# Order of VectorE's work in a slot that holds a pair of heads: the convolution moved behind the weights and the former pair's outputs

## The chip, the cores and the metric

One core of one Trainium2 chip runs the kernel. The metric is device time in microseconds (us) of one launch, the median of several runs; lower is better.

## The reference

One step of a hybrid decoder layer over a prompt of 256 tokens and 8 samples of 8 tokens each, 320 tokens in all (`T = 320`), in float32. After a SwiGLU feed-forward block, a projection `w_in` feeds two branches: an mLSTM and a Mamba-2 scan (SSD). Both are merged, projected, and followed by a second feed-forward block. The change is in the SSD branch:

```python
xbc, sconv1 = _causal_conv(xbc, sconv0, p['s_conv_w'], p['s_conv_b'])   # 4 taps, 3072 channels
xbc = jax.nn.silu(xbc)            # x (2048 channels), B and C (4 groups x 128 each)
...
cum = jnp.cumsum(dtc * A, axis=1)
lmat = jnp.exp(jnp.where(mask, cum[:, :, None] - cum[:, None, :], -jnp.inf))
xdt = xc * dtc[..., None]
cb = jnp.einsum('btgn,bsgn->btsg', cc, bc)
y = (jnp.einsum('btsg,btsge,bsgep->btgep', cb, lmat, xdt)
     + jnp.exp(cum)[..., None] * jnp.einsum('btgn,bgepn->btgep', cc, h))
h_new = (jnp.exp(cum[:, -1])[..., None, None] * h
         + jnp.einsum('bsgn,bsge,bsgep->bgepn', bc, decay, xdt))
```

There are 32 heads of 64 channels in 4 groups of 8 heads; the state has 128 columns. Two heads share one tile of 128 channels, a *pair*, so a group is four pairs.

## The kernel before

**Layout.** Activations lie channels-first, 128 channels a tile on the partitions and 320 tokens in the free dimension. Weights stream from HBM in panels of 1 MB through a ring of four buffers (`ring`), two *units* to a panel. A unit is one tile of 128 output channels.

**A dense unit** (`dense`, L841) multiplies in two halves for float32 accuracy. ScalarE rounds the unit's weights to `w_hi` (`high_ahead`, L1512, instruction L1522), VectorE computes the rest `w_lo` (`low_ahead`, L2076, instruction L2085), and TensorE does 8 matmuls `w_hi` by `u_hi`, 8 `w_hi` by `u_lo`, and 8 `w_lo` by `u_hi`, all through L820. Both halves have two buffers and are made two units ahead: in the slot of unit u, ScalarE waits until TensorE is done with u, then makes the high half of u+2, and VectorE follows with the low half of u+2. A ring buffer is refilled by SyncE once the last low half of its panel is made.

**Groups and slots.** While the SSD scan of a group runs, the remaining units of the projection run between its steps. The loop `for gr in range(SG)` with an inner loop over the eight units of a phase (`phase_units`) stands, in the same shape, in the program of every engine: TensorE L1388, ScalarE L1941, GpSimd L771, VectorE L2669. One pass of the inner loop is a *slot*, i = 0 to 7. There is no planner: each engine's program order is written out by hand, and engines meet on semaphores. In groups 0, 1 and 2 the units of slots 0 to 3 are `xbc` units, which need a convolution; in group 3 these are `gb` units, which need none. Slots 4 to 7 hold `ga` or `z` units (a gate).

**What each engine does in a slot:**
- TensorE: the dense unit; in slot 0 the transposes of the group's inputs and the B-by-C scores (`group_rows`, L1278); in slots 0 to 3 the decay rows of pair i (`decay_rows`, L1304, two matmuls of 448 columns into `aux`); in slot 1, for gr > 0, the transposes of the old part; in slot 2 the growth factors (`grown_decays`, from L2609's tile); in slots 1 to 4 the outputs of pair i - 1 (`head_outputs`, L1316), which wait for that pair's weights (`w_ready`); in slots 4 to 7 the state work (`sample_states`, L1350). The first of these, in slot 4, waits for VectorE to have read all four pairs' outputs (`y_read`), since the state updates go into the same PSUM banks 2 and 3.
- ScalarE: the high half; in an `xbc` slot the copy of the unit's result from PSUM into a padded row `pad2` (L1508; three buffers, reused after the convolution three units before is done); in slots 0 to 3 the exponentials of pair i from `aux` into `w_int` (`head_weights`, L1912, instructions L1923 to L1925, twice); four slots after each `xbc` unit its SiLU (`conv_silu`, L1661), from `acc2` (four buffers).
- GpSimd: history columns and tails of the padded row (`conv_side`, L656), and the selectors of the next pair (`picks`, L762).
- VectorE: the low half (L2085); `conv` (L2241): four chained instructions over 344 columns, L2253, twice L2255, L2257, into `acc2`; in slot 0 `group_rows` (L2580, instructions L2587 to L2594) and `masked_scores` (L2612, L2618 to L2621); in slot 1 `old_part` (for gr > 0; L2664, L2666) and `sample_masks` (L2597; L2602, L2604, and L2609, which feeds TensorE's growth factors); in slots 0 to 3 `weights` of pair i (L2623; L2630 and L2632, which wait for the exponentials and signal `w_ready`); in slots 1 to 4 `outputs` of pair i - 1 (L2635; L2638, signals `y_read`); from slot 4 on `weighted_inputs` (L2644), `update` of the states (L2653) and `gated` (L2525).

`conv` waits for the unit's PSUM bank to be copied out (`bank_free`), for GpSimd's history columns (`hist_put`) and for the SiLU of the unit four before (`conv_silu`).

Of the kernel before, what the change touches and what calls it, by code (L numbers as in the profile page):

```python
# [78 lines left out]
class Stream:  # L79
# [44 lines left out]
    def range(self, first, last):  # L124

        return self.units[self.at[first].n:self.at[last].n + 1]
# [55 lines left out]
def build(nc, io, out):  # L182
# [5 lines left out]
    with ctx:  # L188
# [93 lines left out]
        def part(off, *shape):  # L282
            n = 1
            for s in shape:
                n *= s
            used[0] = max(used[0], off + n)
            assert off + n <= ARENA, off + n
            v = arena[:, off:off + n]
            if len(shape) == 2:
                v = v.rearrange("p (a b) -> p a b", b=shape[1])  # L290
            if len(shape) == 3:
                v = v.rearrange("p (a b c) -> p a b c", b=shape[1], c=shape[2])
            return v
# [63 lines left out]
        pad2 = part(17920, 3, PADW)  # L357
        acc2 = part(18961, 4, PADW)
# [112 lines left out]
        def place(u):  # L471

            return u.own if u.name == "qk" else 16 + (u.own + 8) % 24

        def phase_units(gr):
            return [st.at[name, q] for name, q in four_each(PHASE_UNITS[gr])]
# [1585 lines left out]
        def _(dve):  # L2062
# [13 lines left out]
            def low_ahead(u, last=units[-1]):  # L2076

                done = sum(1 for v in units[:u.n + 1] if v.split)
                while lows[0] < min(done + AHEAD, len(st.split_units)):
                    v = st.split_units[lows[0]]  # L2080
                    if v.n > last.n:
                        break
                    r = v.split_no % 2
                    dve.wait_ge(S["hi_done"], v.split_no + 1)
                    V.tensor_tensor(w_lo[r][:, 0:v.kc, :], panel_part(v), w_hi[r][:, 0:v.kc, :].bitcast(FP32), ALU.subtract)\  # L2085
                        .then_inc(S["lo_done"], 1)
                    lows[0] += 1
# [153 lines left out]
            def conv(u, padded, depth, accs, b_col, w_col, tiles):  # L2241
                own, c = u.own, place(u)
                r = (c - (0 if u.name == "qk" else 16)) % depth
                dve.wait_ge(bank_free[u.bank], u.freed)
                dve.wait_ge(S["hist_put"], c + 1)
                if c >= 4:
                    dve.wait_ge(S["conv_silu"], c - 3)
                a, p = accs[:, c % 4, 0:CONVW], padded[:, r, :]
                if u.name == "qk":
                    dve.wait_ge(S["tap_done"], c + 1)  # L2250
                c = own
                if u.name != "qk":
                    ch.link(V.tensor_scalar(a, p[:, 0:CONVW], par[:, c + w_col:c + w_col + 1], par[:, c + b_col:c + b_col + 1], ALU.mult, ALU.add))  # L2253
                for tap in (1, 2):
                    ch.link(V.scalar_tensor_tensor(out=a, in0=p[:, tap:tap + CONVW], scalar=par[:, c + w_col + tap * tiles:c + w_col + tap * tiles + 1],  # L2255
                                                   in1=a, op0=ALU.mult, op1=ALU.add))
                V.scalar_tensor_tensor(out=a, in0=p[:, 3:3 + CONVW], scalar=par[:, c + w_col + 3 * tiles:c + w_col + 3 * tiles + 1],  # L2257
                                       in1=a, op0=ALU.mult, op1=ALU.add).then_inc(S["conv_done"], 1)
# [263 lines left out]
            def gated(u, dst):  # L2522
                dve.wait_ge(bank_free[u.bank], u.freed)
                c = one(dst, u.own)
                V.tensor_tensor(c, c, one(gate_tmp, gate_no[u.n] % 2), ALU.mult).then_inc(S["gate_used"], 1)  # L2525
# [46 lines left out]
            for q in XBC_FIRST:  # L2572
                u = st.at["xbc", q]
# [6 lines left out]
            def group_rows(gr):  # L2580

                dt = sp[:, :, 4 + 8 * gr:12 + 8 * gr].unsqueeze(3)
                if gr > 0:
                    dve.wait_ge(S["ph_mm"], gr)
                for blk in range(2):
                    dve.wait_ge(S["xt_mm"], 3 * gr + blk + 1)
                    V.tensor_tensor(xd[:, blk, :].rearrange("p (e q) -> p e q", q=64), aux[2 + blk][:, :].rearrange("p (e q) -> p e q", q=64),  # L2587
                                    dt[:, blk].to_broadcast([128, 8, 64]), ALU.mult).then_inc(S["xt_read"], 1)
                dve.wait_ge(S["xt_mm"], 3 * gr + 3)
                if gr > 0:  # L2590
                    dve.wait_ge(S["up_mm"], 4 * gr)
                x = banks[2][0:64, :].rearrange("p (e q) -> p e q", q=64)
                V.tensor_tensor(xd_s[0:64, :].rearrange("p (e q) -> p e q", q=64), x, dt[0:64, 2].to_broadcast([64, 8, 64]), ALU.mult).then_inc(S["xt_read"], 1)
                V.tensor_tensor(xw_s[0:64, :].rearrange("p (e q) -> p e q", q=64), x, sp2[0:64, 2, 8 * gr:8 * gr + 8].unsqueeze(2).to_broadcast([64, 8, 64]),  # L2594
                                ALU.mult).then_inc(S["xt_read"], 1)
# [16 lines left out]
            def masked_scores(gr):  # L2612

                dve.wait_ge(S["cb_mm"], gr + 1)
                if gr > 0:
                    dve.wait_ge(S["w_ready"], 4 * gr)
                blocks = banks[3][:, 0:384].rearrange("p (c t) -> p c t", t=128)
                ch.inc(V.tensor_tensor(cbm[:, 0:384].rearrange("p (c t) -> p c t", t=128)[:, 0::2, :], blocks[:, 0::2, :],  # L2618
                                       tri_m.unsqueeze(1).to_broadcast([128, 2, 128]), ALU.mult))
                ch.inc(V.tensor_copy(cbm[:, 128:256], banks[3][:, 128:256]))  # L2620
                V.tensor_tensor(cbm[0:64, 384:448], banks[3][0:64, 384:448], tri_sm, ALU.mult).then_inc(S["cb_read"], 1)  # L2621
# [13 lines left out]
            def outputs(gr, i):  # L2635
                c = 4 * gr + i
                dve.wait_ge(S["y_mm"], c + 1)
                V.scalar_tensor_tensor(out=xbc_t[:, c, :], in0=xbc_t[:, c, :], scalar=h_dec[:, 128 + c:129 + c], in1=banks[2 + i % 2][:, 0:T],  # L2638
                                       op0=ALU.mult, op1=ALU.add).then_inc(S["y_read"], 1)

            def weighted_inputs(gr):
                dve.wait_ge(S["y_mm"], 4 * gr + 4)
                x = xd[:, :, :].rearrange("p c (e q) -> p c e q", q=64)
                V.tensor_tensor(x, x, sp2[:, 0:2, 8 * gr:8 * gr + 8].unsqueeze(3).to_broadcast([128, 2, 8, 64]), ALU.mult).then_inc(S["xw_ready"], 1)  # L2644
# [13 lines left out]
            def old_part(gr):  # L2658

                dve.wait_ge(S["yi_tr"], gr + 1)  # L2660
                dve.wait_ge(S["grown_read"], gr + 1)
                y = xbc_t[:, 4 * gr:4 * gr + 4, TP:T].rearrange("p t (g s) -> p g t s", g=2)
                o = y_int[:, :, :].rearrange("p g (t s) -> p g t s", s=32)
                ch.link(V.tensor_tensor(o, aux[3][:, 0:256].rearrange("p (g t s) -> p g t s", g=2, s=32),  # L2664
                                        grown.rearrange("p (t g s) -> p g t s", g=2, s=32), ALU.mult))
                V.tensor_tensor(y, y, o, ALU.add).then_inc(S["yi_add"], 1)  # L2666
                dve.wait_ge(S["yi_add"], gr + 1)

            for gr in range(SG):  # L2669
                for i, u in enumerate(phase_units(gr)):  # L2670
                    low_ahead(u)
                    if u.name == "xbc":
                        conv(u, pad2, 3, acc2, 216, 240, 24)
                    if i == 0:
                        group_rows(gr)
                        masked_scores(gr)
                    if i == 1:
                        if gr > 0:
                            old_part(gr - 1)
                        sample_masks(gr)  # L2680
                    if i < 4:
                        weights(gr, i)
                    if 1 <= i <= 4:
                        outputs(gr, i - 1)
                    if i == 4:
                        weighted_inputs(gr)
                    if i >= 4:
                        update(gr, i - 4)
                        gated(u, ya if u.name == "ga" else xbc_t)
# [111 lines left out]
```

## Time and profile before

| | |
|---|---|
| median of 3 runs | 1363.53 us |
| lowest, highest | 1362.2, 1368.29 us |
| the profiled execution: time, span | 1357.09 us, 1355.3 us |
| its mean granted TensorE clock | 0.979 of full speed |
| TensorE (PE) busy | 1278.2 us |
| VectorE (DVE) busy | 767.9 us |
| ScalarE (ACT) busy | 617.8 us |
| GpSimd (POOL) busy | 216.4 us |

The span runs from the first to the last instruction of the one execution that was profiled; its time has the launch around it as well. Times in rows below are us from the start of the span. The four groups of the SSD scan lie at about 727 to 789, 789 to 845, 845 to 900 and 900 to 956 us. The last five lines are shares of one execution with many stages; what a wait in one stage costs has to be read in that stage.

How the rows are read: a timeline row gives start, duration, engine, line, operation, the tile written and the tiles read with their shapes, how many instructions are merged (x), and in brackets how long the engine sat idle before it and which instruction released it. PE is TensorE's matmul queue and PEld its weight loads. All matmuls of the kernel have line 820 and all transposes line 817, as they go through one helper. Tiles that are cut from one large allocation all have the name `arena`; PSUM tiles are `bank` and `aux`. An instruction's shown end can lie a few hundredths of a microsecond behind the start of the next on the same engine.

### The profile page before, as it was taken

To read this page: it belongs to the slowest core of one execution; us is meant where nothing else is said; L and a number is where in the kernel's file an instruction comes from. 1 tells how busy PE (TensorE), PEld (TensorE's weight loads), DVE (VectorE), ACT (ScalarE), POOL (GpSimd) and SP (SyncE) were. 2 spreads that over 40 slices of the span, in tenths; PEclk is the share of its full clock that TensorE was granted. 3 is DMA by queue.
4 is the path that set the end of the run, shared out by engine and by line. 5 is a ranking of instruction groups with operands and counts; after the bars stand their busy time and mean duration, and the time that the engine had idled before them with its cause. 6 is when DMAs were issued, how large, how long until landed. Compare 5 with 4: busy or idle time off the path is not lost.

```text
span 1355.3 us, 22662 instructions
## 1 busy us (share of the span) xinstructions
PE 1278.2 (94%) x9096; PEld 1161.7 (86%) x9096; DVE 767.9 (57%) x1340; ACT 617.8 (46%) x1067; POOL 216.4 (16%) x377
## 2 busy tenths in 40 slices
PE   5899999998999898999999989999999999999997
PEld 2799999997988666778998878788899979999997
DVE  1644445336874455755389676865466565545433
ACT  3433334334667454544355664554563343333342
POOL 4100000002541211111033232321410010000010
PEclk9899999998999999999999999999989999999998
DMA  9957776785332778783673435463335465444551
GB/s 306 257 187 229 234 229 197 226 244 165 124 110 94 250 263 296 253 283 119 173 218 125 139 119 166 138 210 118 116 97 156 155 198 172 141 145 136 150 148 41
DMA packets 258862, 241.56 MB, mean 178 GB/s; under 512 B 8607, under 2 KB 242479, under 8 KB 258710
## 3 DMA queue, kind: packets, MB, share of 16 engines
q1 hardware_dynamic: 249262, 211.03, 50.7%
q0 software_dynamic: 9024, 28.91, 6.1%
q8 instruction: 73, 1.20, 0.4%
q10 hardware_dynamic: 472, 0.17, 0.1%
q14 instruction: 31, 0.25, 0.1%
HBM read 209.88 MB, written 30.21 MB: 177 GB/s over the span
## 4 chain that ended last, share of the span: by engine, by line
PE 57%; DVE 5%; ACT 4%; issue 3%; POOL 1%; DMA 1%; ACTq 0%; DVEq 0%; POOLq 0%
PE bank L820 50%; PE aux L820 6%; ACT w_hi L1522 1%; ACT arena L1508 1%; DVE w_lo L2085 1%; PE aux L817 1%; DVE arena L2255 1%; POOL arena L789 1%; PE bank L817 0%; DMA arena<-in_state_mlstm_C 0%; DMA out_p_C<-arena 0%; ACT L1876 0%; ACT arena L1876 0%; DVE arena L2587 0%; DVE arena L2630 0%
## 5 line engine op out<-in xcount | busy, mean ns | idle before, releaser
L2085 DVE TENSOR_TENSOR w_lo<-ring,w_hi 128x1024 fp32r<-128x1024 f32 (+1 forms) x264 | 336.9, 1277 | 427.9 <-ACT w_hi L1522 427.6
L1522 ACT ACTIVATE w_hi<-ring 128x1024 fp32r<-128x1024 f32 (+1 forms) x264 | 289.4, 1097 | 554.7 <-PE bank L820 548.9
L820 PE MATMUL bank<-u_hi,w_hi 128*128 128x320 f32 x1536 | 277.7, 324 | 6.9 <-ACT u_hi L1547 5.1
L820 PEld LDWEIGHTS bank<-u_hi,w_hi 128*128 128x128 f32 x1536 | 240.5, 195 | 24.5 <-issue 18.8
L820 PE MATMUL bank<-u_lo,w_hi 128*128 128x320 f32 x1536 | 259.1, 312 | 0.0
L820 PE MATMUL bank<-u_hi,w_lo 128*128 128x320 f32 x1536 | 256.6, 309 | 0.0
L820 PEld LDWEIGHTS bank<-u_lo,w_hi 128*128 128x128 f32 x1536 | 236.6, 190 | 0.0
L820 PEld LDWEIGHTS bank<-u_hi,w_lo 128*128 128x128 f32 x1536 | 233.8, 188 | 0.0
L622 POOL TENSOR_TENSOR arena<-arena 128x320 f32<-128x320 f32 x24 | 21.0, 874 | 607.7 <-ACT arena L1534 596.7
L817 PE MATMUL aux<-ident,arena 128*128 128x128 f32 (+6 forms) x404 | 60.3, 274 | 15.9 <-ACT arena L1579 8.8
L820 PE MATMUL bank<-arena 32*128 32x128 f32 (+5 forms) x536 | 55.2, 377 | 16.5 <-issue 6.8
L817 PEld LDWEIGHTS aux<-ident,arena 128*128 128x128 f32 (+6 forms) x404 | 45.1, 142 | 26.9 <-issue 15.1
L820 PE MATMUL bank<-ff_hi,w_hi 128*128 128x320 f32 x352 | 58.5, 314 | 0.0
L820 PEld LDWEIGHTS bank<-arena 32*128 32x128 f32 (+3 forms) x536 | 29.8, 155 | 32.6 <-issue 20.4
L820 PE MATMUL bank<-ff_lo,w_hi 128*128 128x320 f32 x352 | 56.8, 309 | 0.0
L820 PE MATMUL bank<-ff_hi,w_lo 128*128 128x320 f32 x352 | 56.8, 309 | 0.0
L820 PEld LDWEIGHTS bank<-ff_hi,w_hi 128*128 128x128 f32 x352 | 52.3, 188 | 2.5 <-issue 2.5
L820 PEld LDWEIGHTS bank<-ff_hi,w_lo 128*128 128x128 f32 x352 | 52.9, 188 | 0.0
L820 PEld LDWEIGHTS bank<-ff_lo,w_hi 128*128 128x128 f32 x352 | 52.9, 188 | 0.0
L2255 DVE SCALAR_TENSOR_TENSOR arena<-arena,par 128x344 f32<-128x344 f32 x80 | 46.5, 581 | 7.3 <-POOL arena L669 5.1
L820 PE MATMUL aux<-arena 128*32 128x128 f32 (+3 forms) x360 | 46.7, 345 | 4.0 <-ACT arena L1508 3.1
L1508 ACT ACTIVATE arena<-bank 128x256 f32<-128x256 f32 (+4 forms) x138 | 44.4, 352 | 11.9 <-PE bank L820 8.5
(362 smaller groups left out, 1515.4 us busy)
## 6 DMA issues: line engine op xcount, KB each, us to landing
ring<-in_w_in SPq DMA_DIRECT2D x52, 1024.0 KB, 5.1
ring<-in_ff_w SPq DMA_DIRECT2D x44, 1024.0 KB, 5.3
ring<-in_ada_w SPq DMA_DIRECT2D x36, 1024.0 KB, 7.8
ring<-in_ff_w SPq DMA_DIRECT2D x32, 704.0 KB, 4.7
arena<-in_state_mlstm_C SPq DMA_DIRECT2D x32, 512.0 KB, 4.3
out_s_C<-arena POOLq DMA_DIRECT2D x32, 512.0 KB, 4.8
ring<-in_w_pa SPq DMA_DIRECT2D x8, 1024.0 KB, 7.6
arena<-in_state_ssm SPq DMA_DIRECT2D x32, 256.0 KB, 3.4
```

Of the source, the lines that this page charges most:

```text
L622: ins = nc.gpsimd.tensor_tensor(sq[:, 0, :], sq[:, 0, :], sq[:, kc, :], ALU.add)
L789: ch.link(nc.gpsimd.tensor_tensor(gsq[gr][:, 0:2, :], gsq[gr][:, 0:2, :], gsq[gr][:, 2:4, :], ALU.add))
L817: return nc.tensor.transpose(dst, src, ident[0:rows, 0:rows])
L820: return nc.tensor.matmul(dst, lhs, rhs, start=first, stop=last)
L1508: return nc.scalar.activation(dst, src, ACT.Copy, scale=scale)
L1522: nc.scalar.activation(w_hi[v.split_no % 2][:, 0:v.kc, :], panel_part(v), ACT.Copy).then_inc(S["hi_done"], 1)
L2085: V.tensor_tensor(w_lo[r][:, 0:v.kc, :], panel_part(v), w_hi[r][:, 0:v.kc, :].bitcast(FP32), ALU.subtract)\
L2255: ch.link(V.scalar_tensor_tensor(out=a, in0=p[:, tap:tap + CONVW], scalar=par[:, c + w_col + tap * tiles:c + w_col + tap * tiles + 1], in1 ...
```

## The change

In VectorE's slot the convolution no longer stands behind the low half but behind the outputs of the former pair. Nothing else is changed; no instruction is added or removed.

```diff
@@ -2669,8 +2669,6 @@
             for gr in range(SG):
                 for i, u in enumerate(phase_units(gr)):
                     low_ahead(u)
-                    if u.name == "xbc":
-                        conv(u, pad2, 3, acc2, 216, 240, 24)
                     if i == 0:
                         group_rows(gr)
                         masked_scores(gr)
@@ -2682,6 +2680,8 @@
                         weights(gr, i)
                     if 1 <= i <= 4:
                         outputs(gr, i - 1)
+                    if u.name == "xbc":
+                        conv(u, pad2, 3, acc2, 216, 240, 24)
                     if i == 4:
                         weighted_inputs(gr)
                     if i >= 4:
```

## Rows read from the trace of the kernel before

**Rows 1.** The page's first part: busy us, share of the span, instructions.

```profile
PE 1278.2 (94%) x9096; PEld 1161.7 (86%) x9096; DVE 767.9 (57%) x1340; ACT 617.8 (46%) x1067; POOL 216.4 (16%) x377
```

**Rows 2.** Source view of L2632, then L2638, 728 to 875: waits for them (us, times).

```profile
  PE bank L820: 5.5, 8
...
  PE bank L820: 0.9, 3
```

**Rows 3.** Timeline of TensorE, second group, slots 1 to 5.

```profile
798.33 0.87 PE L820 MATMUL bank<-arena 128*64 128x256 f32 x8 [1.06 <-DVE arena L2632]
...
803.92 0.69 PE L820 MATMUL aux<-w_lo_rest,parity 32*128 32x256 f32 x2 [0.34 <-DVE w_lo_rest L2609]
804.99 0.87 PE L820 MATMUL bank<-arena 128*64 128x256 f32 x8 [0.38 <-DVE arena L2632]
...
815.60 0.87 PE L820 MATMUL bank<-arena 128*64 128x256 f32 x8 [0.58 <-DVE arena L2632]
...
818.05 1.16 PE L820 MATMUL bank<-arena 32*128 32x128 f32 x16 [0.28 <-DVE arena L2638]
...
819.71 1.44 PE L820 MATMUL bank<-u_hi,w_hi 128*128 128x320 f32 x8
```

**Rows 4.** Timeline of TensorE, first group, slots 1 and 4.

```profile
737.49 0.87 PE L820 MATMUL bank<-arena 128*64 128x256 f32 x8 [0.88 <-DVE arena L2632]
...
753.90 0.87 PE L820 MATMUL bank<-arena 128*64 128x256 f32 x8 [0.57 <-DVE arena L2632]
...
756.35 1.16 PE L820 MATMUL bank<-arena 32*128 32x128 f32 x16 [0.29 <-DVE arena L2638]
```

**Rows 5.** Timeline of VectorE: slot 0 of the first group, slots 0 to 4 of the second.

```profile
729.59 1.23 DVE L2085 TENSOR_TENSOR w_lo<-ring,w_hi 128x1024 fp32r<-128x1024 f32 x1 [1.58 <-ACT w_hi L1522]
...
790.51 1.22 DVE L2085 TENSOR_TENSOR w_lo<-ring,w_hi 128x1024 fp32r<-128x1024 f32 x1 [5.92 <-ACT w_hi L1522]
791.65 0.47 DVE L2253 TENSOR_SCALAR arena<-arena,par 128x344 f32<-128x344 f32 x1
...
793.88 1.28 DVE L2587 TENSOR_TENSOR arena<-aux,sp 128x512 f32<-128x512 f32 x2
...
797.12 0.96 DVE L2630 SCALAR_TENSOR_TENSOR arena<-arena 128x768 f32<-128x768 f32 x1
...
811.03 1.23 DVE L2085 TENSOR_TENSOR w_lo<-ring,w_hi 128x1024 fp32r<-128x1024 f32 x1 [0.75 <-ACT w_hi L1522]
...
816.22 1.23 DVE L2085 TENSOR_TENSOR w_lo<-ring,w_hi 128x1024 fp32r<-128x1024 f32 x1 [0.21 <-ACT w_hi L1522]
817.36 0.54 DVE L2638 SCALAR_TENSOR_TENSOR arena<-arena,h_dec,bank 128x320 f32<-128x320 f32 x1
```

**Rows 6.** Timeline of ScalarE: last exponentials of slots 0 (first, second group) and 3.

```profile
734.90 0.31 ACT L1925 ACTIVATE arena<-aux,g 64x64 f32<-64x64 f32 x1
...
795.34 0.31 ACT L1925 ACTIVATE arena<-aux,g 64x64 f32<-64x64 f32 x1
...
812.68 0.32 ACT L1925 ACTIVATE arena<-aux,g 64x64 f32<-64x64 f32 x1
```

**Rows 7.** Timeline of the fourth group: VectorE in slot 0, TensorE in slot 4.

```profile
906.68 0.96 DVE L2630 SCALAR_TENSOR_TENSOR arena<-arena 128x768 f32<-128x768 f32 x1 [0.90 <-ACT arena L1925]
...
927.05 1.16 PE L820 MATMUL bank<-arena 32*128 32x128 f32 x16 [0.93 <-DVE arena L2638]
```

**Rows 8.** Windows: length, busy us (x) of PE, PEld, DVE, ACT, POOL, PEclk, DMA, GB/s.

```profile
726.00:732.50 6.50, 4.30 (x30) 3.52 (x29) 4.75 (x8) 2.76 (x8) 3.23 (x8) 1.00 0.51 163
...
770.20:773.80 3.60, 2.12 (x26) 1.76 (x23) 2.25 (x6) 3.31 (x5) 0.08 (x1) 1.00 0.62 176
773.80:777.20 3.40, 3.40 (x25) 2.72 (x26) 1.44 (x6) 2.29 (x4) 1.50 (x2) 0.50 1.02 298
```

**Rows 9.** Timeline of TensorE, first group, slot 6.

```profile
773.80 1.15 PE L820 MATMUL aux<-arena 128*32 128x128 f32 x16 [1.48 <-ACT arena L1508]
774.88 2.48 PE L820 MATMUL bank<-u_hi,w_hi 128*128 128x320 f32 x8
```

## The prediction

> **What bounds the kernel now.** The page's first part comes first: TensorE is busy 94% of the span, VectorE 57% [rows 1], so a VectorE order can only matter where TensorE stands still for it. The source view of the two VectorE lines that TensorE waits for here says how much that is: over the three groups whose slots hold a convolution it waits 5.5 us in 8 waits for the weights (L2632) and 0.9 us in 3 for the outputs (L2638) [rows 2]. The timeline places them. In the second group (gr 1) TensorE waits 1.06 us in slot 1, 0.34 and 0.38 us in slot 2 (first for the decay rows of L2609, then for the weights), nothing in slot 3, and 0.58 and 0.28 us in slot 4 [rows 3]; in the first group 0.88, 0, 0, then 0.57 and 0.29 us [rows 4]. The third group's weights waits are what is left of 5.5 us, 5.5 - 0.88 - 0.57 - 1.06 - 0.38 - 0.58 = 2.0 us, so it repeats the second, and I take its L2609 wait as 0.34 too. All together: first group 1.74, second and third 2.64 each, 7.0 us in all.
>
> The VectorE timeline says why [rows 5]. From the split-off low half at 790.51 to the outputs of pair 3 at 817.36 it runs back to back except for two gaps, 0.75 and 0.21 us, each while it waits for ScalarE's high half. VectorE has hardly any slack in slots 0 to 4.
>
> **What the change moves.** Twelve convolutions (three groups, slots 0 to 3) of four instructions: from the start of the first to the start of what follows, 793.88 - 791.65 = 2.23 us each [rows 5]. Nothing is added or removed; no DMA and nothing of another engine moves. In slot 0 the convolution goes behind the group's rows, the masked scores and the weights; in slot 1 behind the old part, the masks, weights and outputs; in slots 2 and 3 behind weights and outputs. Everything it used to precede starts up to 2.23 us earlier, unless another thing is late next.
>
> Late next: the weights need ScalarE's exponentials. *Slot 0, second group.* Group rows would start at 791.65, and the step from their start to the weights is 797.12 - 793.88 = 3.24 us, so the weights could start at 794.89; but the last exponential ends at 795.34 + 0.31 = 795.65 [rows 6]. So they start at about 795.70: 1.42 us earlier than 797.12, with a new wait of 0.81 us. The fourth group, which has no convolution and so already has the new order, shows this wait: 0.90 us before its first weights [rows 7]. TensorE's 1.06 us in slot 1 goes whole. *Slot 1.* No new wait: the exponentials of pair 1 were made long before. The low half comes first, then the old part, masks and L2609, which end 1.42 us earlier, as do the weights of pair 1. TensorE is itself 1.06 us earlier, so of its 0.72 us in slot 2 0.36 go (1.42 - 1.06) and 0.36 stay. TensorE now runs 1.42 us earlier. *Slots 2 and 3.* The low half of slot 3 stays at about 811.0 (its gap of 0.75 closes, the new wait of slot 0 takes its place), and the weights follow it directly, at 811.0 + 1.1 = 812.1, one convolution earlier than now; their exponentials, earlier by TensorE's 1.42 us, end at 812.68 + 0.32 - 1.42 = 811.6 [rows 6], in time. The 0.58 us of slot 4 goes: TensorE is 2.00 us earlier.
>
> *Slot 4 is where it is given back.* There TensorE, after its transposes, waits for the outputs of pair 3, because the state updates overwrite the same PSUM banks. Those outputs come after the low half of slot 4, and that after convolution 3. So before the outputs of pair 3 stands the same VectorE work as before, in another order, and their time moves only by the change in its waits. Before: the gaps of 0.75 and 0.21 us; as an instruction starts some 0.07 us before the last one's shown end where nothing is waited for, they cost 0.82 and 0.28, together 1.10 us. After: both close, since the convolution fills them, and the 0.80 us in slot 0 is new. Outputs of pair 3: 817.36 - 1.10 + 0.80 = 817.06, 0.30 us earlier. TensorE reaches this wait 2.00 us earlier and leaves it 0.30 us earlier: the wait grows from 0.28 to 0.28 + 2.00 - 0.30 = 1.98 us. The third group is the same. *First group:* the low half starts at 729.59 [rows 5], group rows could start 1.14 later at 730.73, weights 3.24 later at 733.97, but the exponentials end at 734.90 + 0.31 = 735.21 [rows 6]; new wait about 1.28 us. The two gaps there are as in the second, cost 1.1. Outputs of pair 3: 0.17 us later; TensorE arrives 0.88 + 0.57 = 1.45 us earlier and the wait grows from 0.29 to 0.29 + 1.45 + 0.17 = 1.91 us.
>
> **Sum:** +0.17 - 0.30 - 0.30 = -0.4 us, against the profiled execution's 1357.1 us: 1356.7. That execution is 6.4 us below the median of the three runs, 1363.53; the difference of 0.4 us carried over gives **1363.1 us**.
>
> Costed at nothing, with the cover: the low halves of slots 1 to 3 start up to 1.3 us later (first group, slot 1), but each is for the unit two slots on, and a slot is over 5 us; cover gone, it would cost that 1.3 us once a group. SyncE refills a ring buffer after its last low half, so its loads leave as much later, into a ring of four panels with eight units in it. GpSimd and ScalarE reuse the padded rows three convolutions later, and the SiLU of a convolution comes four slots on. Each has more than a slot over against at most 5 us. Bounds: the wait on the exponentials could be 0 at best (group rows slower to start) and 1.3 us at worst in all three, which gives -0.8 x 2 - 1.28 = -2.9 us more on one side and +1.0 us on the other.
>
> **A price the sum leaves out: the clock.** The stalls were spread, none over 1.06 us; now one of about 2 us stands in front of small matmuls (32 rows). Two stretches bear on it. From 726.00 to 732.50 TensorE was busy 4.30 of 6.50 us, with a long wait inside, and its granted clock stayed 1.00 (2.4 GHz). From 770.20 to 773.80 it was busy 2.12 of 3.60 us, and the clock then stood at 0.50 (1.2 GHz) for the 3.4 us to 777.20 [rows 8]. Just before that fall stood a wait of 1.48 us beside small matmuls, and a second stretch like it, some 10 us on, went the same way. The new slot 4 has a wait of 1.98 us and then the small matmuls of the row at 818.05 [rows 3]. Price of one fall: eight dense matmuls took 2.48 us [rows 9] where 1.44 us is usual [rows 3], at least 1.0 us; 3.4 us at half speed lose 1.7 us, the upper end.
>
> The Trainium skill, "TensorE: Matmul & The Clock Gate", section "HAM oscillation — how this bites in real kernels", warns that an array left waiting between bursts is throttled again and the next tile starts cold. That speaks against this change; the trace agrees at 773.8 and not in the stretch from 726. [...]
>
> **Rivals.**
> 1. *Waits swapped, clock holds* (forecast): -0.4 us, 1363.1 us. For it: the VectorE work before pair 3's outputs is the same. Chance 0.48.
> 2. *Clock falls, the slower side.* Place: slot 4 of one to three groups, at the long wait for pair 3's outputs. It decides from a wait like the 1.48 us ones on; before, none in slot 4 is over 0.93 us. One fall: -0.4 + 1.0 = +0.6; three: -0.4 + 3 x 1.7 = +4.7 us; 1364.1 to 1368.2 us. For it: both falls. Against: the 6.5 us stretch that held, and the head outputs and transposes just before the new wait. Chance 0.38.
> 3. *Gain kept.* If the wait for pair 3's outputs does not stretch. It has a floor: in the fourth group, with no convolution, TensorE still waits 0.93 us there [rows 7], since high half, low half and outputs follow one another. So at most 7.0 - 3 x 0.93 = 4.2 us: 1359.3 us. Against it: convolution 3 is in front of that chain. Chance 0.12.
> 4. *The change does nothing:* one engine executes in program order, so the rows must move; only 0.02 that compiled order differs: 1363.5 us.
>
> **Numbers.** No case comes to 0.5% (6.8 us, about what a measurement of this kernel can tell from no change). Only the runs' own scatter does: 1362.2 to 1368.3 among the three, 1357.1 for the profiled one. So same 0.93; faster 0.03 (case 3 and a low median); slower 0.04 (case 2 with three falls and a high one). Range: from case 3 less some scatter, 1358.0, to case 2's top and some scatter, 1370.0.
>
> **What would show it.** Right: in the changed profile TensorE's waits for L2632 fall from 5.5 to under 1.5 us and those for L2638 rise from 0.9 to about 5.9 us, one near 2 us in slot 4 of each of three groups; VectorE waits for L1925 before the first weights, 0.8 to 1.3 us; the fourth group unchanged. The stretch from the first transposes of a group to the first dense matmul of slot 5 (789.16 to 819.71 in the second) is the same within 0.5 us, or 1.0 to 1.7 us longer with a granted clock below 1.00. Wrong: waits for L2638 that stay at 0.3 to 0.9 us, a new wait for the convolutions on ScalarE or GpSimd, or low halves that TensorE waits for.

## The result and the profile after

| | before | after |
|---|---|---|
| median | 1362.2 us (13 runs, 1356.7 to 1368.3) | 1369.9 us (13 runs, 1358.4 to 1376.4) |
| ratio, 95% interval | | 1.0057 (1.0039 to 1.0076) |
| profiled execution, span | 1355.3 us | 1364.3 us |
| its granted clock | 0.979 | 0.976 |

The change makes the kernel slower by 0.57%, some 7.7 us; the forecast was -0.4 us.

The source view of the same two VectorE lines as in [rows 2], changed kernel, first to third group; who waited (us, times):

```profile
  PE bank L820: 0.8, 2
...
  PE bank L820: 6.5, 3
```

The waits for the weights (L2632) fell from 5.5 to 0.8 us, and those for the outputs (L2638) rose from 0.9 to 6.5 us. The timeline of TensorE, changed kernel, slots 1 to 5 of the second group and a bit of the first and third (columns as in [rows 3]):

```profile
757.78 1.16 PE L820 MATMUL bank<-arena 32*128 32x128 f32 x16 [2.16 <-DVE arena L2638]
...
797.36 0.87 PE L820 MATMUL bank<-arena 128*64 128x256 f32 x8
...
803.81 0.87 PE L820 MATMUL bank<-arena 128*64 128x256 f32 x8 [0.38 <-DVE arena L2632]
...
813.77 0.87 PE L820 MATMUL bank<-arena 128*64 128x256 f32 x8
...
818.08 1.74 PE L820 MATMUL bank<-arena 32*128 32x128 f32 x16 [2.15 <-DVE arena L2638]
819.74 1.08 PE L820 MATMUL aux<-arena 128*32 128x128 f32 x16
820.76 2.50 PE L820 MATMUL bank<-u_hi,w_hi 128*128 128x320 f32 x8
823.06 2.33 PE L820 MATMUL bank<-u_lo,w_hi 128*128 128x320 f32 x8
...
876.51 2.08 PE L820 MATMUL bank<-arena 32*128 32x128 f32 x16 [2.15 <-DVE arena L2638]
```

The waits of 1.06, 0.34 and 0.58 us in [rows 3] are gone, 0.38 us stays, and 0.28 us has become 2.15 us, once in each group. The new part stands behind that wait: in the second group the eight dense matmuls at 820.76 take 2.50 us, where the row at 819.71 in [rows 3] has 1.44. The windows view of the changed kernel (columns as in [rows 8]) has the clock: 1.00 during the wait, 0.53 and 0.50 in the two stretches after it, and 1.00 in the first group, whose wait was as long:

```profile
757.80:762.00 4.20, 4.20 (x49) 3.88 (x50) 3.53 (x10) 1.48 (x3) 0.30 (x1) 1.00 0.01 4
814.70:818.30 3.60, 1.45 (x16) 1.18 (x16) 3.53 (x6) 3.44 (x7) 0.00 (x0) 1.00 0.70 243
818.30:821.80 3.50, 3.50 (x36) 2.86 (x35) 2.71 (x9) 0.00 (x0) 0.00 (x0) 0.53 0.00 0
821.80:825.20 3.40, 3.40 (x15) 3.40 (x14) 0.61 (x2) 0.00 (x0) 1.50 (x2) 0.50 0.34 100
```

VectorE, changed kernel, first group, slot 0, the end of slot 3 and slot 4: the convolution is off the front, and the weights wait for the exponentials instead.

```profile
734.76 0.21 DVE L2621 TENSOR_TENSOR arena<-bank,w_lo_rest 64x64 f32<-64x64 f32 x1
736.34 0.96 DVE L2630 SCALAR_TENSOR_TENSOR arena<-arena 128x768 f32<-128x768 f32 x1 [1.38 <-ACT arena L1925]
...
753.76 0.45 DVE L2253 TENSOR_SCALAR arena<-arena,par 128x344 f32<-128x344 f32 x1
...
755.96 1.22 DVE L2085 TENSOR_TENSOR w_lo<-ring,w_hi 128x1024 fp32r<-128x1024 f32 x1
757.09 0.54 DVE L2638 SCALAR_TENSOR_TENSOR arena<-arena,h_dec,bank 128x320 f32<-128x320 f32 x1
```

The last three rows are the order that was foreseen: convolution 3, the low half, and only then the outputs that TensorE waits for.

### The profile page after: what moved, and what is told of

Read it like the earlier page. It is cut to its first block and busy times, and to the rows that moved or that the text cites. A ratio compares the mean times of both kernels' runs of the same rounds, so it can differ in the third digit from the quotient of the medians.

```text
span 1364.3 us, 22662 instructions
## 1 busy us (share of the span) xinstructions
PE 1282.2 (94%) x9096; PEld 1165.6 (85%) x9096; DVE 768.3 (56%) x1340; ACT 617.7 (45%) x1067; POOL 209.4 (15%) x377
## 5 line engine op out<-in xcount | busy, mean ns | idle before, releaser
L1508 ACT ACTIVATE arena<-bank 128x256 f32<-128x256 f32 (+4 forms) x138 | 44.4, 352 | 11.9 <-PE bank L820 8.5
```

The costliest lines, as they stand in the source:

```text
L1508: return nc.scalar.activation(dst, src, ACT.Copy, scale=scale)
```

## The experiments

Two numbers are used for each kernel beside its ratio: the mean granted clock over its runs, and from it the time that half speed costs. A mean clock of c over T us means T x (1 - c) us lost, an estimate from above, since half speed during a wait costs nothing. For the kernel before this is 1362.1 x (1 - 0.9781) = 29.8 us (35 runs, beside the first four experiments), for the changed one 1369.4 x (1 - 0.9744) = 35.1 us (13 runs). So of the 7.3 us between these means 5.3 us is clock. The stretches below are called *the groups*, from the first transposes of the first group to the end of TensorE's first wait for one of GpSimd's group sums (728.66 to 959.98 before, 729.76 to 966.01 in the changed kernel), and *the tail*, from there to the end of the span. The time also follows the clock from run to run: of the 13 of the changed kernel the fastest (1358.4 us) had the highest clock, 0.981, and the slowest (1376.4 us) 0.972.

**Filler in the wait.** TensorE, in `sample_states`, first three groups:

```diff
                 if j == 0:
+                    if gr < SG - 1:
+                        nxt = phase_units(gr)[5]
+                        pe.wait_ge(bank_free[nxt.bank], nxt.uses)
+                        for _ in range(12):
+                            mm(bank_of(nxt), u_hi[:, 0, 0:128], u_hi[:, 0, :])
                     pe.wait_ge(S["y_read"], 4 * gr + 4)
```

> The changed kernel, with 12 filler matmuls (320 columns, into the PSUM bank of the next unit, overwritten by it) in TensorE's program just before its wait for pair 3's outputs in slot 4 of the first three groups. Twelve take about 1.8 us where the wait is 2.15 us, so they hide in it. Theory A (the long wait makes the granted clock fall, the waits themselves are only swapped): the clock stays 1.00 through slot 4 and the time comes back to that of the kernel before within 2 us (ratio 1.000, -0.4 to +1 us). Theory B (the loss of 7.7 us is in waits or in other engines' work, whatever the clock): ratio stays near 1.0057.

Measured: 1360.1 us, ratio 0.998 (0.9966 to 0.9993), mean clock 0.9790. VectorE's program is that of the changed kernel; only what TensorE does while it waits is different. Its timeline, first group, slot 4 (five lines more in the file, so L2643 is the outputs' L2638):

```profile
756.76 2.01 PE L820 MATMUL bank<-u_hi 128*128 128x320 f32 x12
759.08 1.16 PE L820 MATMUL bank<-arena 32*128 32x128 f32 x16 [0.31 <-DVE arena L2643]
760.17 0.65 PE L820 MATMUL aux<-arena 128*32 128x128 f32 x16
760.74 1.43 PE L820 MATMUL bank<-u_hi,w_hi 128*128 128x320 f32 x8
```

The state matmuls come as late as before the filler went in, yet the dense ones behind them run at 1.43 us, and no slot 4 in this profile has a clock below 1.00. The whole loss is gone. Theory B falls: its 1.0057 is far outside the interval. The time is even 1.9 us below that of before, where theory A's sum has -0.4 us. Of the 9.6 us between the means of this kernel and the changed one 6.5 us are clock (35.1 - 28.6); the other 3 us are taken up below.

**The wait in another place.** VectorE, slot 3's convolution put back:

```diff
                     low_ahead(u)
+                    if u.name == "xbc" and i == 3:
+                        conv(u, pad2, 3, acc2, 216, 240, 24)
...
-                    if u.name == "xbc":
+                    if u.name == "xbc" and i < 3:
                         conv(u, pad2, 3, acc2, 216, 240, 24)
```

> The changed kernel, but the convolution of slot 3 stands where it was, behind the low half; slots 0 to 2 keep the new order. VectorE has the same work in front of pair 3's outputs, so TensorE's total wait in slot 4 stays about 2 us, but 1.9 us of it should stand before the head outputs (L2632), behind dense matmuls, and almost none before the small state matmuls. Theory A' (it takes a long wait joined to the small matmuls for the clock to fall): time within 2 us of before. Theory A'' (any wait of 2 us in this stretch is enough): ratio 1.004 to 1.006. Theory B: ratio 1.0057.

Measured: 1362.95 us, ratio 1.001 (0.9995 to 1.0025), mean clock 0.9785. TensorE's timeline, second group, slot 4:

```profile
820.42 0.87 PE L820 MATMUL bank<-arena 128*64 128x256 f32 x8 [2.00 <-DVE arena L2632]
821.22 0.33 PE L820 MATMUL bank<-arena,xd_s 64*64 64x64 f32 x4
821.48 1.10 PE L817 MATMUL aux<-ident,arena 128*128 128x128 f32 x8
822.56 1.16 PE L820 MATMUL bank<-arena 32*128 32x128 f32 x16
823.65 0.65 PE L820 MATMUL aux<-arena 128*32 128x128 f32 x16
824.23 1.43 PE L820 MATMUL bank<-u_hi,w_hi 128*128 128x320 f32 x8
```

A wait of 2.00 us, nearly as long, but with dense matmuls ahead of it and head outputs and transposes behind. The clock held. So the length alone does not decide; a wait joined to the small state matmuls does what this one does not. In the other two groups it is the same, with waits of 2.02 and 2.00 us. A' is right, A'' wrong.

**Slot 3 alone.** The kernel before, only the convolution of slot 3 moved:

```diff
-                    if u.name == "xbc":
+                    if u.name == "xbc" and i < 3:
                         conv(u, pad2, 3, acc2, 216, 240, 24)
...
+                    if u.name == "xbc" and i == 3:
+                        conv(u, pad2, 3, acc2, 216, 240, 24)
```

> The kernel before with only the convolution of slot 3 moved behind the weights and outputs; slots 0 to 2 in the old order. The weights waits of slots 1 and 2 stay (0.9 to 1.06, 0.34 and 0.38 us), the 0.58 us one of slot 4 goes, and the wait for pair 3's outputs is about 0.9 us instead of 0.28. Theory A: a wait of 0.9 us is as in the fourth group, where the clock held, so the time is that of before within 2 us. Theory B (an inherent cost of running the convolution of slot 3 late, for example for slots 4 to 7): ratio 1.004 or more.

Measured: 1364.4 us, ratio 1.0023 (1.0004 to 1.0041), mean clock 0.9781. Between the two theories, because the wait was mis-sized: 1.48 us, not 0.9, since the weights of slot 3 now wait for their exponentials (0.78 us), a wait that I had left out. Second and third group, slot 4:

```profile
819.64 1.16 PE L820 MATMUL bank<-arena 32*128 32x128 f32 x16 [1.48 <-DVE arena L2638]
...
821.30 1.44 PE L820 MATMUL bank<-u_hi,w_hi 128*128 128x320 f32 x8
...
875.67 1.16 PE L820 MATMUL bank<-arena 32*128 32x128 f32 x16 [1.48 <-DVE arena L2638]
...
877.34 2.13 PE L820 MATMUL bank<-u_hi,w_hi 128*128 128x320 f32 x8
```

The same wait cost a fall in one of these groups and none in the other, nor in the first group, where it is 1.48 us too. The runs' mean clock is not below that of before, so this small loss (2.5 us) is not shown to be the clock's; what else it may be comes below.

**Outputs first in slot 4.**

```diff
+                    if i == 4:
+                        outputs(gr, 3)
                     low_ahead(u)
+                    if i == 4 and us[3].name == "xbc":
+                        conv(us[3], pad2, 3, acc2, 216, 240, 24)
...
-                    if 1 <= i <= 4:
+                    if 1 <= i < 4:
                         outputs(gr, i - 1)
-                    if u.name == "xbc":
+                    if u.name == "xbc" and i < 3:
                         conv(u, pad2, 3, acc2, 216, 240, 24)
```

> The changed kernel, and in slot 4 the outputs of pair 3 go first, ahead of the low half, and the convolution of slot 3 behind that low half. Pair 3's outputs then follow TensorE's head outputs at once, so the wait in slot 4 should be under 0.3 us in every group, the fourth one too, where it was 0.93. Waits that go: about 1.7 us in the first group, 2.3 in the second and third, 0.9 in the fourth. Theory A: 7 us faster than before, ratio 0.995, granted clock not below that of before. Theory B (a late convolution costs by itself): little better than the changed kernel.

Measured: 1356.6 us, ratio 0.9957 (0.994 to 0.9973), mean clock 0.9793. In its profile no TensorE wait for L2638 is left in the four groups, only 0.8 us for L2632. It beats both kernels, and with the convolution later than in either, so a late convolution has no large cost by itself. It is 5.3 us faster, a little less than the 7 expected: in slot 4 of each of the four groups TensorE now waits 0.36 us for ScalarE (L1508), 1.4 us in all that the expectation left out.

**Profiles repeated: the changed kernel twice more, the kernel before once more.**

> The changed kernel unaltered, for a second profile. Theory A1 (the clock falls in slot 4 nearly every time): the granted clock is 0.50 for a stretch right after the wait for pair 3's outputs in at least two of the three groups. Theory A2 (the two falls of the first profile were chance): in none or one.

> The changed kernel unaltered, for a third profile, as the one before: A1 two or three falls in slot 4, A2 none or one.

> The kernel before unaltered, for a second profile. Both theories: no fall in slot 4 of any group. It also shows whether the wait of 2.4 us for GpSimd's second group sum in the tail, which the changed kernel's profile has at 973.96 and that of before has not, goes with the kernel or with where the clock falls: with the kernel, it is absent here; with the clock, it appears when the clock does not fall near the first group sum.

Windows of the second profile of the changed kernel (1368.6 us; first group, second group, third group):

```profile
762.90:766.40 3.50, 2.41 (x24) 2.20 (x28) 2.37 (x5) 2.56 (x5) 0.00 (x0) 0.58 0.00 1
766.40:769.80 3.40, 3.40 (x26) 3.00 (x18) 2.27 (x9) 0.00 (x0) 0.96 (x2) 0.50 0.02 5
828.00:832.00 4.00, 4.00 (x33) 3.50 (x30) 2.66 (x10) 0.00 (x0) 0.97 (x2) 0.57 0.00 0
876.00:890.00 14.00, 11.85 (x111) 10.75 (x108) 11.40 (x23) 6.38 (x16) 3.84 (x6) 1.00 0.29 92
```

and of the third (1374.5 us):

```profile
761.50:768.90 7.40, 6.82 (x46) 6.21 (x47) 4.13 (x11) 2.05 (x4) 1.59 (x2) 0.54 0.09 28
826.90:834.20 7.30, 7.30 (x50) 6.66 (x50) 3.38 (x10) 0.00 (x0) 1.50 (x2) 0.53 0.19 56
885.00:892.00 7.00, 6.82 (x47) 6.21 (x48) 3.72 (x11) 0.27 (x2) 1.50 (x2) 0.51 0.11 33
```

Seven of nine slots 4 in three profiles had a fall: two, two, three. Six of these seven lost 3.4 us (two stretches at half speed, 7 us in a row), one lost 1.7 us: 6 x 3.4 + 1.7 = 22.1 us, 7.4 us an execution. The second profile of the kernel before (1360.7 us) had none, as the first. A1 is right. The execution with the most falls is the slowest of the three.

This is not the net cost. The waits of 1.48 us in slots 6 and 7 of the first group had a fall of 1.7 us in four of four places before and in four of six in the changed kernel, 1.1 us an execution less. In all, the groups took 231.3 and 231.6 us before and 236.3, 234.5 and 240.5 us in the changed kernel, 5.7 us more in the mean; the tail took 395.3 and 395.7 us, then 398.3, 396.3 and 398.1 us, 2.1 us more. The stretch ahead of the groups, where the two kernels have the same program, differs by 3.1 us between these means too, so such means of two and three executions are good to a few microseconds.

**More filler.** The kernel of outputs first, with the same kind of filler (9 matmuls in slots 6 and 7 of the first group, 10, 12 and 18 ahead of the three waits for group sums in the tail; `filler` waits for the bank and issues the matmuls, and its definition is left out here):

```diff
...
+                if gr == 0 and j >= 2:
+                    filler((phase_units(0) + phase_units(1))[4 + j + 1], 9)
...
+                    filler(tail_units()[2], 10)
                     group_sums(0)
...
                     group_sums(1)
+                    filler(tail_units()[3], 12)
                     group_sums(2)
...
+                    filler(tail_units()[6], 18)
                     group_sums(3)
```

> The kernel of outputs first in slot 4, and in TensorE's program filler matmuls (as in the filler run, 1.3 to 2.7 us in all each time) ahead of the other long waits of this stretch: slots 6 and 7 of the first group (wait 1.48 us each) and the three waits for GpSimd's group sums in the tail (1.5, up to 2.4, 2.85 us). The fillers compute nothing that is used. Theory A (a long wait costs its own length and a fall of the clock behind it, and matmuls in the wait prevent the fall): four falls fewer of 1.7 us each, so about 6 us less than outputs first alone: 1350 us, ratio 0.991, clock up by 0.005. Theory B (the clock falls do not matter to the time here, other work hides them): 1356 us as before.

Measured: 1354.6 us, ratio 0.9948 (0.9922 to 0.9973), mean clock 0.9835. The falls went, none is left in the groups or near the group sums: the clock is up by 0.0042, 5.7 us. But the time is only 2.0 us below that of outputs first, inside both intervals (1.0 us if each is set against the kernel before beside it). So some 4 us of the 5.7 do not show in the time: theory A's 0.991 lies outside the interval, and theory B's 1356 us inside. What the falls in slots 6 and 7 and in the tail cost is therefore not shown by this run. In the tail of its profile TensorE waits 2.2 us for ScalarE to read a bank (in two waits), which the profile of outputs first has not; but that of the one-group kernel below, which has no filler, has it too, so this is not shown to be the filler's doing. This kernel is no proven gain over outputs first.

**The wait halved.** The changed kernel, and in slot 4 `outputs(gr, 3)` ahead of `low_ahead(u)`, nothing else.

> The changed kernel, and in slot 4 only the low half goes behind the outputs of pair 3 (the convolution of slot 3 stays in front of them). The wait for these outputs shrinks by one low half, 2.15 - 1.13 = 1.0 us in the first three groups, and goes in the fourth. Theory A (falls of the clock come with the length of this wait): no or few falls in slot 4, so the waits' own sum remains: -0.4 - 3 x 1.1 - 0.9 = -4.7 us against before, ratio 0.9965, clock as before (0.978). Theory B (a late convolution of slot 3 is what costs): the falls stay and the ratio is 1.002 or more.

Measured: 1359.8 us, ratio 0.9987 (0.9972 to 1.0002), mean clock 0.9772. The wait was as expected, and so was its slot; second group:

```profile
816.61 1.16 PE L820 MATMUL bank<-arena 32*128 32x128 f32 x16 [1.02 <-DVE arena L2638]
817.70 0.65 PE L820 MATMUL aux<-arena 128*32 128x128 f32 x16
818.27 1.43 PE L820 MATMUL bank<-u_hi,w_hi 128*128 128x320 f32 x8
```

No slot 4 of this profile had a fall, and the 7.7 us loss is gone, which B denied. But -4.7 us was not reached, only -1.2 us. In its profile the groups took 226.3 us, 5.2 us less than before, but the tail 399.4 us, 3.9 us more; what that is comes below. The runs' clock was lower than that of before beside them (0.9788), by 0.0016 or 2.2 us. Where those falls are in the runs without a profile is open.

**One group alone.** The new order in the second group, the old one elsewhere (`gr != 1` in front, `gr == 1` behind).

> The new order in the second group only, the old one in the first and third. Theory A: one place for falls instead of three, so about a third of the 7.7 us: +2.5 us, ratio 1.002 (1.000 to 1.003), mean granted clock lower by 0.0012. Theory B (some fixed cost outside the groups, as in the tail): it comes with the first changed group or not at all, ratio 1.000 or 1.0057.

Measured: 1364.5 us, ratio 1.0026 (1.0008 to 1.0044), mean clock 0.9774 against 0.9788 beside it, 0.0014 lower where 0.0012 was expected. One changed group costs 3.6 us, between a third and a half of the three. Its profile happens to show no fall in the slot 4 that was changed, so the reading rests on the runs' clock and time, not on a row. With it the wait of 2.15 to 2.17 us was followed by a fall in seven of ten places. The clock's part here is 1.9 us (1365 x 0.0014); the other 1.7 us is like the rest of the changed kernel below. Both of theory B's values lie outside the interval.

## Why the prediction was wrong

**The moves were right, row by row.** New wait on the exponentials: 1.28, 0.81 and 0.81 us forecast, 1.38 and 0.90 us in the rows (first and second group). TensorE's waits before slot 4: 0 and 0.36 us forecast, 0 and 0.38 measured. The wait for pair 3's outputs: 1.91 and 1.98 us forecast, 2.16 and 2.15 measured. Fourth group: 0.93 us again.

**The sum was close.** From a group's first transposes to the state matmuls of slot 4: 28.02 us (729.76 to 757.78) for 27.69 (728.66 to 756.35) in the first group, 28.76 (789.32 to 818.08) for 28.89 in the second (789.16 to 818.05), and the third likewise. That is +0.3 and twice -0.1 us: +0.1 us in all for -0.4. The missing tenths are mostly low halves in slots 1 and 3 and weights in slot 3, which take 1.31 and 1.04 us where 1.22 and 0.95 us are usual.

**What failed is the step "A price the sum leaves out: the clock", twice.** First its chance: 0.38 for falls against 0.48 for a clock that holds. The stretch from 726 that held was given as much weight as the two that fell; but there the wait has dense matmuls ahead and full transposes behind, as in the conv-3-early kernel, where a 2.00 us wait cost nothing either. The two that fell had the wait beside small matmuls, and that was the likeness to go by. Even their 1.48 us had a fall behind it in 15 of 22 places, over the eleven profiles without filler there. Seven of nine is the measured share for the new wait. Second its price: 1.0 to 1.7 us a fall, from the one pattern in which full speed came back after 3.4 us; its lower end counts only the eight matmuls of one row, and no fall measured here lost less than 1.7 us. Behind the new wait the clock mostly stayed low for 7 us, 3.4 us lost. Rival 2 named the place and the mechanism and topped out at +4.7 us; with the measured price and share, its sum gives -0.4 + 7.4 = +7.0 us. That this comes so near to 7.7 us is in part luck: the groups grew by 5.7 us, as slots 6 and 7 had fewer falls, and the tail by 2.1 us. The tail is the third thing that went wrong: the prediction put everything behind the groups at nothing, without a word on it.

The page that I cited (the Trainium skill, "TensorE: Matmul & The Clock Gate", section "HAM oscillation — how this bites in real kernels") says that the burst after a wait for data starts cold. The wait in its example is one of 3 to 5 us, so it does not reach down to one of 2 us, for which the prediction used it. With that said, this case agrees at 818 and 876, with 2.50 us where 1.44 us is usual, and disagrees at 757.8, behind an equal wait. Had the prediction taken the fall as the likelier case, it would have had the right sign.

**The rest, about 2 us.** Without the lost time the means are 1334.3 us after and 1332.3 us before (35 runs), 2.0 us apart with a standard error of some 0.7 us. A candidate is in the tail of the first profile of the changed kernel, in the wait for GpSimd's group sums (TensorE, then VectorE and GpSimd):

```profile
966.01 0.81 PE L820 MATMUL aux<-ones,arena 128*128 128x1 f32 x6 [1.52 <-POOL arena L790]
...
973.96 0.81 PE L820 MATMUL aux<-ones,arena 128*128 128x1 f32 x6 [2.44 <-POOL arena L790]
974.70 1.84 PE L820 MATMUL bank<-u_hi,w_hi 128*128 128x320 f32 x8
...
971.72 1.47 DVE L2085 TENSOR_TENSOR w_lo<-ring,w_hi 128x1024 fp32r<-128x1024 f32 x1 [2.89 <-ACT w_hi L1522]
972.17 1.73 POOL L790 TENSOR_TENSOR arena<-arena 128x320 f32<-128x320 f32 x1
```

The second wait, 2.44 us, is not in the kernel before. It does not go with the order of VectorE: of three profiles of the changed kernel two have it, and so have slot 3 alone and the wait halved; the other profiles without filler in the tail, both of the kernel before among them, have not.

It goes with the clock: in the seven without it the clock fell right behind the first of these waits, TensorE was slowed, and GpSimd's next sum was ready when it came; in the four with it the clock held there, TensorE ran into the wait, and the clock fell in it or behind it.

The tail of these four took 398.1 to 399.4 us, that of the seven 395.3 to 397.0 us. Part of the wait is a slower sum: the one that TensorE waits for (L790, the row at 972.17) takes 1.73 us in these four and 0.86 or 0.87 us in the seven. In the four a low half of VectorE (the row at 971.72) starts 0.44 or 0.45 us ahead of it and takes 1.46 or 1.47 us; in the seven it starts 1.1 us behind the sum's start, when the sum has ended, and takes 1.23 us. The wait of 2.44 us in two of three profiles explains 1.6 us of the 2. Whether the change makes this case more frequent, or three profiles overstate it, stays open. The same 2.4 us is in the profile of slot 3 alone, whose 2.5 us its mean clock doesn't explain.

## What to carry to other kernels

Gathering several short waits of TensorE into one is not neutral, even when their sum stays the same: look at what stands on both sides of the one that grows. Beside small matmuls a wait of 2 us cost 3.4 us more behind it in six of nine cases and 1.7 us in a seventh; one of 1.48 us there cost 1.7 us in one of three, one of 1.02 us nothing in three; behind dense matmuls and ahead of head outputs and transposes, 2.0 us cost nothing that stands out of the noise (ratio 1.001). Put first on the helper engine what TensorE waits for last in the stretch (here pair 3's outputs, ahead of low half and convolution): that alone, on top of the change, turned +7.7 into -5.3 us.

## What was not expected of the hardware

A fall of the clock to 0.50 lasts 3.4 or 7 us in the groups and the tail, and mostly 7 behind the new wait; the same program has it in one group and not in another, and in one execution and not in the next. That is a large part of what makes runs of one kernel differ: 1358.4 us at a mean clock of 0.981, 1376.4 us at 0.972 is 18 us, of which 12 are 1367 x 0.009.

Half speed can also help later: with a fall behind the first group sum (1.7 us lost) the wait of 2.4 us at the next does not come, in seven of seven profiles.

The lengthened low halves and weights (1.31 and 1.04 us) lie where they now run at the same time as GpSimd's casts of the selectors (L767: 1.75 us for the two from 810.92, 0.95 us for the two from 804.39). The tail has a like pair, GpSimd's sum of 1.73 us and VectorE's low half of 1.46 us, long in each of the five profiles in which they run at the same time (more filler is the fifth) and usual in each of the seven in which they do not. That the two slow each other down is the likely reading; no run here moved only one of them.
